# Attention in a three-block network: the product of weights and values as three fp32r products of split parts, every second block, 256 columns wide

## The reference

```
def block(args):                       # 128 queries of all heads
    qi, start = args
    scores = jnp.einsum("bqhrd,bshrd->bhrqs", qi, k).astype(jnp.float32) * scale
    dist = jnp.abs((start + jnp.arange(Q_BLOCK))[:, None] - k_pos[None, :]).astype(jnp.float32)
    scores = scores - slopes[None, :, None, None, None] * dist[None, None, None]
    probs = jax.nn.softmax(scores, axis=-1)
    w = probs[:, :, 0] - lam * probs[:, :, 1]
    return jnp.einsum("bhqs,bshe->bqhe", w.astype(v.dtype), v)
...
o = rms_norm(o, subln_g) * (1.0 - lam_init)
y_attn = o.reshape(b, s, D_ATTN) * jax.nn.silu(g)
```

## Time and profile before

| | |
|---|---|
| median of 3 runs | 3786.94 us (3786.23 to 3787.26) |
| the profiled execution, its own time | 3784.53 us |
| its span in the profile | 3782.8 us |
| PE busy over the span | 3609.8 us (95%) |
| DVE busy | 2251.6 us (60%) |
| ACT busy | 1668.6 us (44%) |
| attention, scores of block 8 to scores of block 56 (heads 1 to 6) | 498.6 us, 83.1 us a head |

### The profile page before, as it was taken

The page is one execution under the profiler, slowest core; times in us unless marked ns, Lnnn a source line. Parts: engine busy times, 40 slices in busy tenths (PEclk is TensorE's granted clock), DMA queues, the critical chain, the costliest instruction groups (busy, mean ns, idle before and its releaser), DMA issues.

```text
span 3782.8 us, 48362 instructions
## 1 busy us (share of the span) xinstructions
PE 3609.8 (95%) x20222; PEld 3036.7 (80%) x20222; DVE 2251.6 (60%) x2947; ACT 1668.6 (44%) x2123; POOL 468.9 (12%) x373
## 2 busy tenths in 40 slices
PE   8999989999998999999999989999999999999998
PEld 7778968888876787877777759978777888778998
DVE  4545353456666765655656662468889888843332
ACT  4333344431114544467667772145455554442132
POOL 0001032200000121200000000012222222210001
PEclk9999999999999899999999999999999999999999
DMA  3012023342212011011111123121111111153111
GB/s 110 23 40 90 26 81 109 112 159 89 89 69 90 23 34 40 18 51 34 37 28 34 29 86 140 42 82 34 45 45 39 56 51 45 34 213 110 45 40 67
DMA packets 227389, 244.85 MB, mean 65 GB/s; under 512 B 10007, under 2 KB 190180, under 8 KB 227172
## 3 DMA queue, kind: packets, MB, share of 16 engines
q1 hardware_dynamic: 222391, 224.92, 18.4%
q10 hardware_dynamic: 4781, 16.84, 1.2%
HBM read 191.40 MB, written 50.33 MB: 64 GB/s over the span
## 4 chain that ended last, share of the span: by engine, by line
PE 77%; DVE 12%; ACT 5%; issue 3%; DMA 1%; POOL 0%; SPq 0%; ACTq 0%; DVEq 0%; POOLq 0%
PE pd L211 63%; PE pq L211 11%; PE pd L366 2%; DVE t L3520 2%; DVE t L328 1%; DVE t L3528 1%; PE pq L366 1%; DVE t L3965 1%; ACT t L3125 1%; ACT t L320 1%; DVE t L3952 0%; DVE t L3950 0%; DVE t L3197 0%; DVE t L2078 0%; DVE t L3215 0%
## 5 line engine op out<-in xcount | busy, mean ns | idle before, releaser
L211 PE MATMUL pd<-t 128*128 128x512 f32 (+2 forms) x15104 | 2904.1, 353 | 32.5 <-ACT t L3716 9.8
L211 PEld LDWEIGHTS pd<-t 128*128 128x128 f32 x15104 | 2407.6, 191 | 459.8 <-issue 90.9
L211 PE MATMUL pq<-t 128*128 128x128 f32 (+5 forms) x3782 | 635.7, 330 | 75.0 <-DVE t L4001 15.7
L211 PEld LDWEIGHTS pq<-t 128*128 128x128 f32 (+2 forms) x3782 | 484.3, 181 | 187.4 <-issue 44.4
L320 ACT ACTIVATE t<-t 128x2048 fp32r<-128x2048 f32 (+3 forms) x133 | 212.6, 1599 | 633.2 <-PE pd L211 590.8
L328 DVE TENSOR_TENSOR t<-t 128x2048 fp32r<-128x2048 f32 (+3 forms) x133 | 257.3, 1935 | 173.7 <-ACT t L320 173.2
L1919 DVE TENSOR_TENSOR t<-pd,t 128x512 f32<-128x512 f32 x256 | 172.9, 689 | 104.9 <-PE pd L211 102.7
L3248 DVE COPY t<-pd 128x512 f32<-128x512 f32 x64 | 44.2, 691 | 218.6 <-PE pd L366 218.6
L3528 DVE SCALAR_TENSOR_TENSOR t<-t 128x1024 f32<-128x1024 f32 x120 | 173.8, 1448 | 0.5
L3520 DVE SCALAR_TENSOR_TENSOR t<-t 128x1024 f32<-128x1024 f32 x120 | 169.1, 1409 | 2.1
L3917 POOL TENSOR_TENSOR t<-t 128x512 f32<-128x512 f32 x56 | 96.0, 1714 | 592.8 <-ACT t L3861 299.4
(11 more groups left out here) (345 smaller groups left out, 2830.8 us busy)
## 6 DMA issues: line engine op xcount, KB each, us to landing
t<-in_w_in_dram SPq DMA_DIRECT2D x97, 512.0 KB, 4.3
t<-in_w_out_dram SPq DMA_DIRECT2D x20, 1024.0 KB, 5.4
t<-in_w_in_dram SPq DMA_DIRECT2D x16, 1024.0 KB, 5.3
t<-in_w_mlp_dram SPq DMA_DIRECT2D x64, 256.0 KB, 3.5
u_scratch<-t SPq DMA_DIRECT2D x64, 256.0 KB, 3.3
t<-in_w_mlp_dram SPq DMA_DIRECT2D x16, 1024.0 KB, 5.0
t<-u_scratch SPq DMA_DIRECT2D x15, 1024.0 KB, 7.2
t<-in_x_dram SPq DMA_DIRECT2D x16, 512.0 KB, 9.2
```

The lines of the kernel that those rows point to most:

```text
L211: ins = e.matmul(out, l, r, start=(first and j == 0), stop=(last and j == n - 1), skip_group_check=True)
```

## The change

The product with the values is made from split parts, as the other products are. Four things move with that:

- The weights' buffer WT (8 x 512 float32) becomes two buffers of 8 x 256 in fp32r, a high and a low part, so the product is made every second block for 256 queries: four times a head, at places 0, 2, 4 and 6, 24 matmuls of 256 columns each.
- ACT now writes the high part of both transposed halves (two copies), and DVE writes both low parts (two subtractions), each of which waits for ACT's copy of the same half. Before, ACT copied the one half and DVE the other, both waiting for PE alone.
- The transposed values are split likewise: ACT copies, DVE subtracts (`dve_att_vt`, new).
- Square and copy of the result come four times a head with 256 columns instead of twice with 512; `tmp` grows from 4 to 6 buffers; the region that the output projection's inputs come back into is now a raw tile under the high part of the values.

The core of the diff:

```diff
-    WT = sbt(ph, [128, 8, 512])
-    tmp = ring(ph, 4, [128, 512])
+    WT = [sbt(ph, [128, 8, 256], F32R) for _ in range(2)]
+    tmp = ring(ph, 6, [128, 512])
...
+    def dve_att_vt(e, h, th):
+        sl = slice(th * 4, th * 4 + 4)
+        e.wait_ge(*at["avh", h, th])
+        if h >= 2:
+            e.wait_ge(*at["AV", h - 2, 3])
+        e.tensor_tensor(AB[h % 2][2][:, sl, :], four(PD.of("avT", h, th)[:, :]), AB[h % 2][1][:, sl, :].bitcast(F32),
+                        SUB).then_inc(*at.inc("dve", "avt", h, th, free=("avT", h, th)))
...
-        for m in range(n, n + 4):
+        for m in range(n, n + 2):
             for q2 in range(2):
                 e.wait_ge(*at["wTc", m, q2])
...
-        mms(e, b[:, :], [(AB[h % 2][1][:, j, :], WT[:, j, :]) for j in range(8)]).then_inc(*at.inc("pe", "AV", h, th))
+        _, vh, vl, _ = AB[h % 2]
+        mms(e, b[:, 0:256], [p for j in range(8) for p in three(vh[:, j, :], vl[:, j, :], WT[0][:, j, :],
+                                                                WT[1][:, j, :])]).then_inc(*at.inc("pe", "AV", h, q))
...
-            if tt % 4 == 0 and n:
-                pe_att_values(e, n - 4, next(turns))
+            if tt % 2 == 0 and n:
+                pe_att_values(e, n - 2, next(turns))
...
-        pe_att_values(e, 60, next(turns))
+        pe_att_values(e, 62, next(turns))
...
-        e.activation(q[:, :], b[:, :], ACT.Square).then_inc(*at.inc("act", "osq", h, th))
-        e.copy(o[:, :], b[:, :]).then_inc(*at.inc("act", "o", h, th, free=("AV", h, th)))
+        e.activation(q[:, c], b[:, 0:256], ACT.Square).then_inc(*at.inc("act", "osq", h, th))
+        e.copy(o[:, c], b[:, 0:256]).then_inc(*at.inc("act", "o", h, th, free=("AV", h, q4_)))
...
-            e.wait_ge(*at["wT", n, 0])
-            e.copy(WT[:, 0:4, tile(tt % 4)], four(PD.of("wT", n, 0)[:, :])).then_inc(
-                *at.inc("act", "wTc", n, 0, free=("wT", n, 0)))
+            for q2 in range(2):
+                e.wait_ge(*at["wT", n, q2])
+                e.copy(WT[0][:, q2 * 4:q2 * 4 + 4, tile(tt % 2)], four(PD.of("wT", n, q2)[:, :])).then_inc(
+                    *at.inc("act", "wTh", n, q2))
...
-            e.wait_ge(*at["wT", n, 1])
-            if tt % 4 == 0 and n:
-                e.wait_ge(*at["AV", h if tt else h - 1, 0 if tt else 1])
-            e.tensor_copy(WT[:, 4:8, tile(tt % 4)], four(PD.of("wT", n, 1)[:, :])).then_inc(
-                *at.inc("dve", "wTc", n, 1, free=("wT", n, 1)))
+            if tt >= 6 and h < 7:
+                dve_att_vt(e, h + 1, tt - 6)
+            if tt % 2 == 0 and n:
+                e.wait_ge(*at["AV", h if tt else h - 1, (tt // 2 + 3) % 4])
+            for q2 in range(2):
+                sl = slice(q2 * 4, q2 * 4 + 4)
+                e.wait_ge(*at["wTh", n, q2])
+                e.tensor_tensor(WT[1][:, sl, tile(tt % 2)], four(PD.of("wT", n, q2)[:, :]),
+                                WT[0][:, sl, tile(tt % 2)].bitcast(F32), SUB).then_inc(
+                    *at.inc("dve", "wTc", n, q2, free=("wT", n, q2)))
```

More of the change, by code:

```diff
@@ L2859, in program @@
     KL = [[WL[2][:, 1024:2048], sbt(ph, [128, S], F32R)], [sbt(ph, [128, S], F32R) for _ in range(2)]]
-    AB = [[sbt(ph, [128, S]), sbt(ph, [128, NT, 128])] for _ in range(2)]
+    AB = []
+    for _ in range(2):
+        raw = ExitStack()
+        gT32 = sbt(raw, [128, S])
+        v32 = sbt(raw, [128, NT, 128])
+        raw.close()
+        AB.append([sbt(ph, [128, S]), sbt(ph, [128, NT, 128], F32R), sbt(ph, [128, NT, 128], F32R), v32])
     SR = ring(ph, 3, [128, 2, S])
-    WT = sbt(ph, [128, 8, 512])
-    tmp = ring(ph, 4, [128, 512])
+    WT = [sbt(ph, [128, 8, 256], F32R) for _ in range(2)]
+    tmp = ring(ph, 6, [128, 512])
     sm = ring(ph, 4, [128, 8])
@@ L2920, in act_att_out @@
     def act_att_out(e, h, kind, th):
-        gT, vt_ = AB[h % 2]
+        gT = AB[h % 2][0]
         sl, b = half(th), PD.of("a" + kind, h, th)
@@ L2952, in act_att_vt @@
         if h >= 2:
-            e.wait_ge(*at["AV", h - 2, 1])
+            e.wait_ge(*at["AV", h - 2, 3])
         e.copy(AB[h % 2][1][:, th * 4:th * 4 + 4, :], four(PD.of("avT", h, th)[:, :])).then_inc(
-            *at.inc("act", "avt", h, th, free=("avT", h, th)))
+            *at.inc("act", "avh", h, th))
+    def dve_att_vt(e, h, th):
+        sl = slice(th * 4, th * 4 + 4)
+        e.wait_ge(*at["avh", h, th])
+        if h >= 2:
+            e.wait_ge(*at["AV", h - 2, 3])
+        e.tensor_tensor(AB[h % 2][2][:, sl, :], four(PD.of("avT", h, th)[:, :]), AB[h % 2][1][:, sl, :].bitcast(F32),
+                        SUB).then_inc(*at.inc("dve", "avt", h, th, free=("avT", h, th)))
     def dve_att_out(e, h, kind, th):
@@ L3012, in pe_att_values @@
     def pe_att_values(e, n, bank):
-        h, th = n // 8, n // 4 % 2
-        b = at_bank(e, bank, "AV", h, th)
-        for m in range(n, n + 4):
+        h, q = n // 8, n // 2 % 4
+        b = at_bank(e, bank, "AV", h, q)
+        for m in range(n, n + 2):
             for q2 in range(2):
@@ L3077, in back_in @@
     def back_in(k):
-        return [KL[0][1].bitcast(F32), flat(AB[0][1])][k % 2]
+        return [KL[0][1].bitcast(F32), flat(AB[0][3])][k % 2]
     def sp_o2_fetch(e, k):
@@ L3085, in sp_o2_fetch @@
         else:
-            e.wait_ge(*at["AV", 6, 1])
+            e.wait_ge(*at["AV", 6, 3])
         e.dma(back_in(k)[:, :], YM[k * 128:(k + 1) * 128, :], "y2a", k)
@@ L3111, in act_att_values @@
     def act_att_values(e, n):
[L3112 to L3116, removed]
-        e.activation(q[:, :], b[:, :], ACT.Square).then_inc(*at.inc("act", "osq", h, th))
-        e.copy(o[:, :], b[:, :]).then_inc(*at.inc("act", "o", h, th, free=("AV", h, th)))
+        h, q4_ = n // 8, n // 2 % 4
+        th, c = q4_ // 2, slice(q4_ % 2 * 256, q4_ % 2 * 256 + 256)
+        b = PD.of("AV", h, q4_)
+        o = tmp.of("o", h, th) if q4_ % 2 else e.take(tmp, "o", h, th)
+        q = tmp.of("osq", h, th) if q4_ % 2 else e.take(tmp, "osq", h, th)
+        e.wait_ge(*at["AV", h, q4_])
+        e.activation(q[:, c], b[:, 0:256], ACT.Square).then_inc(*at.inc("act", "osq", h, th))
+        e.copy(o[:, c], b[:, 0:256]).then_inc(*at.inc("act", "o", h, th, free=("AV", h, q4_)))
     def act_stage_att(e):
@@ L3172, in act_stage_att @@
                 act_unit(e)
-        act_att_values(e, 60)
+        act_att_values(e, 62)
         act_att_ms(e, 7, 1)
@@ L3220, in dve_stage_att @@
         dve_unit(e)
+        dve_att_vt(e, 0, 0)
         dve_att_out(e, 0, "k", 0)
+        dve_att_vt(e, 0, 1)
         dve_att_out(e, 0, "k", 1)
```

2 lines of the change are left out of this document (1 added, 1 removed).

## The result

The changed kernel takes 3883.4 us, median of 4 runs (3881.73 to 3886.18); the kernel before takes 3787.1 us in runs of the same time. The ratio is 1.0253, with a 95% interval from 1.0239 to 1.0268: slower, by 96 us. 3879 was forecast.

The account below looks back on a forecast made before the run. PE bounds the kernel before at 83.1 us a head; the change makes the loop of ACT and DVE serial. 3784.5 + 72 (loop) + 20 (clock) = 3876.5, with 2.4 to the median 3879 us; range 3835 to 3910.

Parts of the forecast that it names:

- What PE saves: PE's product with the values in split form, 2.88 us four times a head for 6.89 twice: 2.3 us a head saved.
- That both engines have time, and that this doesn't help: ACT and DVE stay under 70 of 83 us a head in sum, but the added wait is what counts.
- The loop: In heads 1 to 6, ACT and DVE no longer run side by side: 91.5 us a head against 83.1, +50 us.
- DVE's part: DVE's work from ACT's copies to ACT's next block, while ACT idles: 24.7 us a head.
- The clock: PE's idle pieces lower its granted clock: 1.7 us at place 6, 0.8 at place 2, 0.5 at place 0, +20 us.
- The bank at place 2: The block's first transposes share a bank with the product and wait for ACT's copy out of it: 0.7 us.
- Head 7: The last head, without projection, where nothing hides anything: +13 us, between +6 and +18.
- Blocks 1 to 7: The same loop ahead of heads 1 to 6, without the mean square at place 2: +8 us.
- the start: Ahead of the loop DVE makes the values' low parts: +0.7 us (0 to 1.4).
- Absorbed: Rival: PE waits at each product for low parts but the next block catches up; 3812 us, chance 0.07.
- faster: Rival: PE stays the bound as ACT and DVE idle enough, so only PE's 18 us count; 3769 us, chance 0.04.
- The loop without the clock: Rival: PE's idle pieces are too short or fall where PE has slack; 3859 us, chance 0.22.

Follow-up runs that it names:

- e2: The changed kernel with DVE's low parts moved behind the next block's mix and reciprocals, weight unit and gating behind the maxima: 3791.07 us.
- e7: The kernel before, with DVE's second-half copy also waiting for ACT's copy, but moved behind the next block's mix and reciprocals: 3784.2 us.
- e6: The changed kernel with DVE's low parts later, ACT's square and copy early at places 0 and 2, and head 7's end reordered on DVE and PE: 3770.15 us.
- e4: The changed kernel with one more DVE subtraction per block, the second half's low part made twice: 3946.48 us.
- e3: The changed kernel with ten idle matmuls on PE ahead of the product at place 6 and of the transposes at place 2, heads 0 to 6: 3875.21 us.
- e5: The changed kernel with ACT's square and copy of the product ahead of the mean square and exponentials at places 0 and 2: 3887.86 us.
- e1: The kernel before with one added wait: DVE's copy of the second transposed half also waits for ACT's copy of the first: 3848.92 us.

## Why the prediction was right

**What PE saves: right.** The product of 24 matmuls starts 2.93 us ahead of what follows it (1803.78 to 1806.71 us in the changed kernel, at full clock), where 2.88 was taken from the earlier trace rows. Once PE is the bound again, a head shrinks by 2.4 us (e2, 83.1 to 80.7), for 2.3 forecast; PE's busy time in the heads fell from 494.22 to 480.33 us, 2.3 a head. Against e7, which has the new order on DVE and the old product, e2 is 1.7 shorter and e6, with ACT's values early, 2.6. The Trainium skill's four passes for true FP32 ("FP8 and Floating Point Precision", TensorE Precision Notes) agree with the rows: 0.86 us for a float32 matmul of 512 columns (6.89/8), 3.8 times the 0.2275 us of one in fp32r (5.46/24). What the rows don't bear out is the saving worked out from them, 10 us larger: a matmul of 256 columns takes 0.120 us (5.76/48), more than half of 0.2275, so three split products cost 0.84 of the float32 one and not three quarters.

**That both engines have time, and that this doesn't help: right.** ACT's busy time is 62.9 us a head, for 62.6. e4 shows that the loop has no slack, e2 and e6 that it is the loop: with equal work the heads fall to 80.7 and 79.9.

**The loop: right in kind, small by 1.1 us a head.** ACT's time in a head of the changed kernel, from rows shown above:

| us a head | forecast | measured |
|---|---|---|
| ACT busy | 62.6 | 377.48/6 = 62.9 |
| waits for reciprocals | 24.7 | 147.1/6 = 24.5 |
| waits for maxima | 1 | 7.3/6 = 1.2 |
| waits for PE at full clock: bank, low parts at places 4 and 6 | 0.7 + 2.4 | 21.4/6 = 3.6 (e3) |
| the clock: what these waits have more than in e3 | 3 | (24.4 + 6.3 - 21.4)/6 = 1.5 |
| not listed | | 0.4 |
| sum | 94.4 | 94.1 |

At full clock (e3) it is 92.6 where 91.5 was forecast: 0.5 in the waits for PE, 0.4 not listed, the rest in ACT's work and the maxima. DVE's part, 24.7, was nearly exact. The block at place 2 was the longest, as forecast, but takes 16.3 us on ACT (e3) and about 17.3 from scores to scores (16.8 in e3), for 15. The prediction's own terms give it: 8.24 to the exponentials, 2.3 for them, 0.6 for square and copy, 0.7 for the bank, 1.1 for the copies and 3.3 for DVE's part with a weight unit are 16.2, so the 15 was added up too low. That the total came so near, 3879 for 3883, is partly luck: in the heads the loop was 6.9 us short (50 for 56.9 at full clock), and the clock term 8.7 too large (18 for 9.3).

**The clock: right that it counts, too large.** The steps were 1.7 us at place 6, 0.8 at place 2, 0.5 at place 0, 3 in all. PE's idle pieces came out about as forecast, 2.88 us at place 2 and 2.78 at place 6, 10.2 a head in all for 11. But their effect was not the same each time. Here is one at place 2, and what followed; the clock is at 0.50 from about 1956.0 to 1959.4:

```profile
1952.29:1955.17 2.88, 0.00 (x1) 0.01 (x1) 0.00 (x0) 2.82 (x7) 0.00 (x0) 1.00 0.00 0
1955.17:1958.60 3.43, 3.43 (x14) 2.95 (x15) 2.05 (x3) 1.16 (x2) 0.00 (x0) 0.62 0.02 5
1958.60:1961.00 2.40, 2.40 (x10) 1.91 (x10) 2.37 (x5) 0.72 (x1) 0.00 (x0) 0.83 0.00 0
```

And one at place 6 (head 1) behind which the product ran at its full speed, 3.10 us for 24 matmuls:

```profile
1803.78 3.10 PE L211 MATMUL pd<-t 128*128 128x256 f32 x24 [2.75 <-DVE t L3272]
1806.71 0.60 PE L366 MATMUL pd<-t 128*128 128x128 f32 x4
```

e3 gives 1.6 us a head, 9.3 over the heads, where 18 were forecast; the granted clock of the heads was 0.97, where the prediction had 0.9 or so. By ACT's blocks against e3, place 6 cost 1.2 a head for 1.7, places 2 and 3 together 0.4 for 0.8, and place 0 nothing for 0.5. At place 6 a fall cost 1.3 to 1.5 us, and 2.7 in head 3, where the lower clock lasted 6.8 us instead of 3.4, but in two heads of six it didn't come. What fails is the step "such a stretch costs 1.7" as a cost in every head.

**The bank at place 2: right.** It was put at 0.7 us in the loop. PE waits 2.88 us for it, but the loop passes through it only where ACT waits for the transposes, 0.75 us; e5, which takes the bank's wait away, has the block at place 2 shorter by 0.72. The rest of PE's 2.88 us was no cost: with the bank free PE waits at the next product instead. That e5 gained nothing in sum is the clock at places 4 and 6.

**Head 7: +16.5, for +13 (6 to 18).** PE idles there in pieces of up to 5.5 us, and its granted clock is 0.83, which was 0.93 before. The transposes that wait for the bank, at place 0 and at place 2; the first line is the kernel before at place 0:

```profile
2229.79 0.66 PE L366 MATMUL pd<-t 128*128 128x128 f32 x4 [0.73 <-ACT t L3118]
...
2307.18 1.11 PE L366 MATMUL pd<-t 128*128 128x128 f32 x4 [5.46 <-ACT t L3135]
...
2328.88 1.97 PE L366 MATMUL pd<-t 128*128 128x128 f32 x8 [5.50 <-ACT t L3135]
```

At place 0 the wait was 0.73 us before, at place 2 it was 3.79. These waits alone are not what costs: in e5 they are 1.78 and 1.34 us, but PE then waits 4.3 and 4.9 us for DVE, and head 7 is only 0.6 us shorter (88.72 us). What the orders together are worth e6 shows: its head 7 takes 77.85 us, 11.5 less.

**The sum.** Blocks 1 to 7 gave +9.4 (forecast +8 and 2 of the clock), the heads +66.2 (+50 and +18), head 7 +16.5 (+13), the start +0.6 (+0.7): +92.7, where I had 92. The two executions are 98.2 us apart, though. The other 5.4 us arise later, between about 3160 and 3470 us of the span before, in code that is the same in both. All seven experiments show about +5 to +7 there against that one execution of the kernel before, also e6 and e7, which are ahead of it until then. That execution, 3784.53 us, is at the low end of its kernel's own runs (3784.5 to 3794.0 in the first set), so I take this as that execution's luck, not as the change's cost; by the medians only 3.6 us are left over. It was not tested.

**The rivals.** *Absorbed* (3812) and *faster* (3769) rested on slack that the loop doesn't have. The condition that I named for *faster*, the reciprocals of a block ready before ACT's copies of the one before, is what the order of e2 and e6 brings about. That e6 measures 3770 is near that rival's price by chance: its heads gained 3.2 us each, more than PE's 2.3, and its head 7 took 5.1 us longer than before the change. *The loop without the clock* (3859) falls by e3, which has the full clock in the heads and takes 3875; and the changed kernel's clock did fall, which e3 puts at 9.3 us.

## What to carry to other kernels

When an edit adds a wait between two engines that each run a fixed order, list what stands behind the wait on its engine and who needs it: the same wait cost 63 us in one place in the row (e1) and nothing that the times show a few instructions later (e7). Busy shares don't show this (60% and 67% here), so write the loop down as one engine's work plus its waits for the other, and compare that with the bound; a gap of a third engine is worth only what the loop waits in it: of PE's 2.88 us at place 2 that was 0.75. And closing it can move the idle time to a place where the clock costs more (e5).

## What the runs showed of the hardware that was not expected

Idle pieces of PE of nearly equal length had different sequels. In the heads of the changed kernel they measured 2.75 to 2.89 us. Each of the six at place 2 had 3.4 us at granted clock 0.50 behind it; of the six at place 6, three had 3.4 us, one 6.8 and two none. After 2.97 us in e5 the clock was at 0.50 for 6.8 us. What tells these apart the rows do not show.

The chip's queues behaved as the Trainium skill says ("TensorE: Matmul & The Clock Gate", Architectural detail: ScalarE and VectorE take their instructions strictly in order); e1 and e7 put a number on it, 65 us.
